# A bias operation in attention that raises one semaphore itself, where it waited for itself and raised two

## The reference

```python
# fox, per block of 128 queries (start..end), keys 0..end
s = jnp.einsum('bqhd,bkhd->bhqk', q[:, start:end], k[:, :end]) * scale
s = s + Ft[:, :, start:end, None] - Ft[:, :, None, :end]
s = jnp.where(tk <= tq, s, -jnp.inf)
p = jax.nn.softmax(s, axis=-1)
outs.append(jnp.einsum('bhqk,bkhd->bqhd', p, v[:, :end]))
# dsa: the same with keys and values of the topk picked positions, and no forget term
```

## Time and profile before

| | us |
|---|---|
| median of 3 runs | 3328.57 (3326.97 to 3331.42) |
| profiled execution, its own time | 3329.86 |
| its span, first to last instruction | 3328.1 |
| attention stage in it, from the first bias operation to the projections | 557 to 866 |
| busy over the span: PE / DVE / ACT / POOL | 3148.4 / 2182.5 / 1333.0 / 998.4 |
| mean granted TensorE clock over the span | 0.977 |

### The profile page before, as it was taken

How to read it: one execution, slowest core, us unless ns; L and a number is a source line. 1 busy time by engine, 2 the same in 40 slices (tenths; PEclk the granted TensorE clock), 3 DMA queues, 4 the chain that set the end, 5 groups by cost and what they waited for, 6 DMA issues and landing times.

```text
span 3328.1 us, 44945 instructions
## 1 busy us (share of the span) xinstructions
PE 3148.4 (95%) x15149; PEld 2514.4 (76%) x15149; DVE 2182.5 (66%) x2721; ACT 1333.0 (40%) x1772; POOL 998.4 (30%) x493
## 2 busy tenths in 40 slices
PE   6999998888999699999969999999999999999998
PEld 6568775555787588888858888888688888888877
DVE  7788877787554899999956775633655155145366
ACT  4345434667312688888841365101411000001142
POOL 2233332000242011111113433345144444444432
PEclk8999998899999799999989999999999999999999
DMA  7223121331151999999971222233211111111312
GB/s 259 70 64 102 56 65 45 109 106 41 61 169 64 371 380 379 380 382 384 343 272 48 67 87 79 65 110 91 106 50 51 51 44 50 48 47 50 108 38 70
DMA packets 351446, 446.19 MB, mean 134 GB/s; under 512 B 32942, under 2 KB 235612, under 8 KB 351332
## 3 DMA queue, kind: packets, MB, share of 16 engines
q1 hardware_dynamic: 336532, 410.05, 36.2%
q10 hardware_dynamic: 5440, 17.86, 1.6%
q0 software_dynamic: 9360, 16.80, 1.3%
HBM read 397.40 MB, written 58.75 MB: 137 GB/s over the span
## 4 chain that ended last, share of the span: by engine, by line
PE 57%; DVE 5%; SPq 2%; DMA 2%; issue 1%; ACT 1%; DVEq 0%; ACTq 0%; POOLq 0%
PE acc L430 14%; PE acc L432 14%; PE acc L431 14%; PE acc L2025 3%; PE acc L2027 3%; PE acc L2026 3%; PE acc L2046 1%; PE acc L2045 1%; PE acc L2044 1%; SPq L1928 1%; DMA mraw<-in_exp_w 1%; PE XX L2016 1%; SPq L1929 1%; DVE Al L709 0%; DMA G<-ys 0%
## 5 line engine op out<-in xcount | busy, mean ns | idle before, releaser
L430 PE MATMUL acc<-Ah,whi 128*128 128x512 f32 x2208 | 872.1, 395 | 7.6 <-DVE Al L718 3.3
L403 POOL TENSOR_TENSOR whi<-wraw,one 128x1024 fp32r<-128x1024 f32 (+1 forms) x199 | 378.5, 1902 | 1657.6 <-PE acc L432 1307.5
L431 PE MATMUL acc<-Al,whi 128*128 128x512 f32 x2208 | 860.6, 390 | 0.0
L432 PE MATMUL acc<-Ah,wlo 128*128 128x512 f32 x2208 | 860.6, 390 | 0.0
L405 POOL TENSOR_TENSOR wlo<-wraw,whi 128x1024 fp32r<-128x1024 f32 (+1 forms) x199 | 517.3, 2599 | 15.6
L430 PEld LDWEIGHTS acc<-Ah,whi 128*128 128x128 f32 x2208 | 414.7, 188 | 114.2 <-issue 16.2
L431 PEld LDWEIGHTS acc<-Al,whi 128*128 128x128 f32 x2208 | 414.7, 188 | 89.3 <-issue 4.1
L432 PEld LDWEIGHTS acc<-Ah,wlo 128*128 128x128 f32 x2208 | 414.5, 188 | 88.2
L2138 DVE TENSOR_TENSOR mlo<-mraw,mhi 128x1024 fp32r<-128x1024 f32 x256 | 307.0, 1223 | 38.0 <-ACT mhi L2082 25.3
L2082 ACT ACTIVATE mhi<-mraw 128x1024 fp32r<-128x1024 f32 x256 | 268.1, 1063 | 74.7 <-PE acc L2027 50.9
L430 PE MATMUL acc<-Bh,whi 128*128 128x512 f32 x640 | 250.0, 391 | 0.0
(11 more groups left out here) (598 smaller groups left out, 5043.4 us busy)
## 6 DMA issues: line engine op xcount, KB each, us to landing
mraw<-in_exp_w SPq DMA_DIRECT2D x512, 256.0 KB
mraw<-in_exp_w SPq DMA_DIRECT2D x128, 512.0 KB, 12.1
wraw<-in_w_in SPq DMA_DIRECT2D x72, 512.0 KB, 3.9
wraw<-in_w_up SPq DMA_DIRECT2D x46, 512.0 KB, 3.8
TT<-in_ada_w SPq DMA_DIRECT2D x32, 512.0 KB, 3.8
TT<-gates SPq DMA_DIRECT2D x32, 512.0 KB, 4.5
wraw<-in_w_down SPq DMA_DIRECT2D x24, 512.0 KB, 3.9
adaraw<-in_ada_w SPq DMA_DIRECT2D x16, 512.0 KB, 8.4
```

The costliest lines, as they stand in the source:

```text
L403: ch(pool.tensor_tensor(hi[:, r, 0:k, 0:m], wraw[:, r, 0:k, 0:m], one[:, 0:1].unsqueeze(2).broadcast_to([P, k, m]), ALU.mult))
L430: pe.matmul(o, hi[:, hr, j, 0:m], ih[:, k0 + j, cols], start=(j == 0), stop=False)
L431: pe.matmul(o, hi[:, hr, j, 0:m], il[:, k0 + j, cols], start=False, stop=False)
L432: last = pe.matmul(o, lo[:, hr, j, 0:m], ih[:, k0 + j, cols], start=False, stop=(j == k - 1))
```

## The change

`biased` no longer goes through `ch`: its instruction raises `s_max` itself when it is done, VectorE does not wait for it, and the two raising instructions go. `scores` waits for `s_max`, by the count at which the two bias operations of the unit before are done; only the first unit still waits for `acc_free`. The last two bias operations still raise `acc_free` by hand, behind a wait for `s_max`, for the projections that follow. No instruction that computes is added, removed or put elsewhere, and no DMA.

```diff
             for e in range(2):
-                pe.wait_ge(acc_free[e], take(e))
+                if u == 0:
+                    pe.wait_ge(acc_free[e], take(e))
+                else:
+                    pe.wait_ge(S("s_max"), 2 * u - 1 + e)
...
-            ch(dve.tensor_tensor_reduce(weights_at(s)[:, 0:w], acc[s % 2][:, 0:w], bias, -SCALE, 3e38, ALU.add, ALU.min,
-                                        nmax(s)))
-            dve.sem_inc(acc_free[s % 2], 1)
-            dve.sem_inc(S("s_max"), 1)
+            dve.tensor_tensor_reduce(weights_at(s)[:, 0:w], acc[s % 2][:, 0:w], bias, -SCALE, 3e38, ALU.add, ALU.min,
+                                     nmax(s)).then_inc(S("s_max"), 1)
+            if s >= 2 * len(units) - 2:
+                dve.wait_ge(S("s_max"), s + 1)
+                dve.sem_inc(acc_free[s % 2], 1)
```

## The result

The changed kernel takes 3302.62 us (median of 4 runs, 3302.03 to 3304.57), beside 3329.70 for the kernel before on the same chip: a ratio of 0.9919, 95% interval 0.9907 to 0.9932. That is 27.1 us less; 21.5 were forecast, and 3302.62 lies in the range of 3292.5 to 3319.5. The profiled execution took 3303.06 us, 26.8 less than the one of before.

The account below looks back on a forecast made before the run. In attention no engine was full; TensorE ended the stage, idle 54.2 us, 30.2 of it waiting for the bias operations. Gains of 3.7 + 4.4 + 7.1 + 6.3 = 21.5 us from 3328.57 gave 3307.1, range 3292.5 to 3319.5.

Parts of the forecast that it names:

- The gaps: VectorE's idle between two bias operations, 0.36 to about -0.08 us, and before the reciprocal, 0.24 to about -0.08.
- The signal: From the accumulator read's end to TensorE's weight load for the scores: 0.18 becomes 0.05 us, 0.13 saved.
- The loop without `ada`: Bias, bias, signal, scores, where the unit's first bias operation waited for scores: saves 0.44 + 0.13 = 0.57 us.
- for each of TensorE's 33 waits, the wait or the saving, whichever is smaller: Gain rule for attention's waits of the scores for the bias operations, 30.2 us in all; summed to 21.5 us.
- ScalarE's copies: Rival: in wide units, half the gain returns as longer TensorE waits for transpose-bank copies; 10.7 us left, 3317.8; chance 0.20.
- some 9: Sign of a right forecast: TensorE's waits for the scores' bank in attention fall from 30.2 to some 9 us.
- The rival in which the clock rises as well: In attention, closing waits also keeps TensorE more at 2.4 GHz; gain put at 32.7 us, 3295.9; chance 0.18.
- the operation's emptying: Rival: the 0.36 us between bias operations is VectorE's own emptying, so nothing is saved; 3328.6; chance 0.06.
- slower: Rival: TensorE in attention is granted 1.2 GHz for longer; at 60 us more, 8.5 us lost, 3337.1; chance 0.04.

Follow-up runs that it names:

- six matmuls more: Kernel before with six short bf16 matmuls added a unit in 24 units, ahead of TensorE's wait for the score banks; 3331.28 us, ratio 1.0001.
- two raises more: Kernel before with two more raising instructions behind each bias operation's self-wait, on a semaphore nobody waits for; 3347.40 us, ratio 1.0056.
- second operation direct: Changed kernel, but only each pair's second bias operation raises the count itself; the first keeps its self-wait and one raising instruction; 3316.52 us, ratio 0.9958.
- self-wait put back: Changed kernel with VectorE again waiting for its own count after each bias operation, the two raising instructions left out; 3307.81 us, ratio 0.9930.
- first operation direct: Changed kernel, but only each pair's first bias operation raises the count itself; the second keeps its self-wait and one raising instruction; 3308.27 us, ratio 0.9933.

## Why the prediction was right, and where its size was off

*The gaps* held to 0.01: -0.08 and -0.08, so VectorE's 0.76 a unit was sized rightly. What the gap consisted of was not asked finely enough: I weighed the self-wait, and most of it was the instructions queued behind it.

*The signal* was taken as 0.18 to 0.05; it became 0.12, so the weight load did not come within the 0.1 that the prediction named as a sign. The loop without `ada` saved 0.51 in the unit shown, not 0.57.

*The term that was mis-sized* is the one that turned VectorE's saving into a gain: "for each of TensorE's 33 waits, the wait or the saving, whichever is smaller". TensorE's waits for VectorE gave 16.3 us, not 21.5, and 2.0 went back to ScalarE's copies; the waits for the scores' bank went to 15.5, not to some 9. The gain was larger all the same, since its busy time, which the sum had taken as fixed, fell by 11.5. That the time fell well inside the range is thus in part luck: the waits alone gave 14.3, just under the forecast's own 15 to 27, and a rival with a chance of 0.18 gave the rest. One head pair shows how. This is the busy time by stretch over the third fox pair, before and after (the stretches start and end at the first bias operation of width 128), and between them TensorE's waits for VectorE before:

```profile
632.40:673.30 40.90, 35.46 (x300) 25.09 (x299) 31.65 (x74) 24.28 (x59) 0.00 (x0) 0.88 0.41 130
```

```profile
PE acc L1334 <- DVEq L1410: 2.9, 5, 0.8
...
PE XX L1351 <- DVE Pb L1417: 0.3, 1, 0.3
```

```profile
624.70:659.90 35.20, 30.64 (x298) 21.89 (x297) 30.23 (x74) 23.59 (x59) 0.00 (x0) 1.00 0.48 150
```

It saved 5.7 us. TensorE had waited for VectorE in it for 2.9 + 0.3 us only, so by my rule it could not save more than 3.2. But VectorE set the pace in nearly all of its eight units, and seven of them became 0.6 to 0.9 shorter, most by 0.76 to 0.78, VectorE's own saving, whatever TensorE's wait had been: its busy time had held slack, matmuls at 1.2 GHz (a granted 0.88) that VectorE's pace covered. When the pace rose, the granted clock was 1.00 and the same matmuls took 4.8 us less. The clock accounts for all of that, by estimate: 0.12 x 2 x 40.9 = 9.8 us had run at 1.2 GHz, and would take half as long at 2.4.

*The rival in which the clock rises as well* thus came in, in part: 0.93 to 0.97 over the stage, which the prediction had named as a sign that the clock made part of the difference. The table has the stage in us, from the first bias operation to the first matmul of the projections: the kernel before, five kernels with other gaps, and the run with six matmuls more.

| | attention | TensorE busy | its waits for VectorE | for ScalarE's copies | clock |
|---|---|---|---|---|---|
| before | 308.5 | 254.3 | 32.7 | 21.2 | 0.93 |
| two raises more | 326.4 | 256.7 | 49.3 | 20.1 | 0.93 |
| second operation direct | 294.2 | 243.8 | 27.3 | 22.9 | 0.97 |
| self-wait put back | 288.7 | 243.9 | 26.6 | 17.6 | 0.97 |
| first operation direct | 286.3 | 240.6 | 26.7 | 18.8 | 0.98 |
| changed kernel | 282.6 | 242.8 | 16.4 | 23.2 | 0.97 |
| six matmuls more | 310.3 | 257.3, 12.5 of it the added ones | 31.7 | 21.1 | 0.96 |

The higher clock and 10 to 14 us less busy time come with every shorter loop, whether it is half the change or the whole. What sets these kernels apart is mostly the waits.

Whether the closed waits raised the clock is not proved. All seven kernels with the shorter loop have 0.97 or 0.98 over the stage, the one with more raising instructions 0.93. The mean clock of every whole run agrees: 0.976 to 0.979 before, 0.980 to 0.984 in the seven. But six short matmuls raised it to 0.96 with the waits in place, and without any gain of time. It would fit that a higher clock is no gain while VectorE sets the pace and a condition of the gain once it does not; no run shows that by itself. A place where the clock may have cost time: the third dsa pair, at 1.00 before, at 0.95 in the changed kernel, and at 1.00 again in the run with only the first operation direct.

```profile
788.60:822.40 33.80, 28.30 (x263) 19.53 (x264) 24.63 (x68) 25.33 (x61) 0.00 (x0) 1.00 0.00 1
```

```profile
764.10:797.70 33.60, 29.10 (x258) 20.12 (x259) 23.33 (x67) 24.96 (x59) 0.00 (x0) 0.95 0.00 1
```

```profile
769.10:801.50 32.40, 27.74 (x259) 19.08 (x260) 23.95 (x67) 25.18 (x61) 0.00 (x0) 1.00 0.00 1
```

There the whole change saved 0.2 us, and half of it 1.4, although VectorE's gaps were longer in that run.

*The other rivals.* ScalarE's copies took back 2.0, not half of the gain. The gap was the waits' and raises', not the operation's emptying: the accumulator read in front overlaps like any other instruction. The kernel did not get slower.

## What to carry to other kernels

An engine that waits for its own operation and then raises semaphores by separate instructions pays for each of them at the end of the operation: here 0.04 and 0.10 apiece, against -0.08 when the operation raises the semaphore itself. Look for it as an idle time that the engine's own last instruction "ended", and count the instructions behind the self-wait. The self-wait can go only where no later instruction of the same engine reads the result without a wait of its own: here VectorE next reads the weights behind its wait for ScalarE's exponentials, and these wait for `s_max`. When you turn such a saving into a gain, do not cap it by the other engine's recorded waits alone: busy time at a lower granted clock is slack too, as long as the clock does rise.

## What the runs showed of the hardware that was not expected

- A self-wait alone leaves 0.04 us between two VectorE instructions, and -0.08 without it: 0.12, where the gap looked like 0.36.
- A raising instruction on VectorE costs about 0.10 us behind a self-wait (two more a bias operation made the kernel 17.3 us slower) and nothing measurable without one (3303.04 and 3302.62 us with and without 256 of them).
- A wide bias operation can start while the accumulator read of the one before it is still running: both start at 636.87.
